# First stage of a decoder trunk reordered: modulation weights before the input rows, input rows in groups of two tiles, projections begun on half the tokens

## What is computed

```python
def rmsnorm(x, g):
    xf = x.astype(jnp.float32)
    y = xf * lax.rsqrt(jnp.mean(xf * xf, axis=-1, keepdims=True) + EPS)
    return (y * g.astype(jnp.float32)).astype(x.dtype)

c_act = jax.nn.silu(c)
for l in range(DEPTH):                                   # DEPTH = 2
    mod = c_act @ w_ada[l] + b_ada[l]                    # 6 rows of 1024
    sh_m, sc_m, g_m, sh_f, sc_f, g_f = [m[:, None, :] for m in jnp.split(mod, 6, axis=-1)]
    h = rmsnorm(x, norm_mix_g[l]) * (1 + sc_m) + sh_m
    if l % 2 == 0:
        z = h @ w_in_even[i]                             # 1024 x 2560
        u, v, b_gate, c_gate, x_in = jnp.split(z, split_pts, axis=-1)
        y_a = chunk_sgu(u, v, sgu_norm_g[i], w_spatial[i], b_spatial[i])
        y_b = short_gated_conv(b_gate, c_gate, x_in, conv_w[i])
        y = jnp.concatenate([y_a, y_b], axis=-1) @ w_out_even[i]
    else:
        y = pool_mixer(h, w_pool[i], pool_scale[i])
    x = x + g_m * y
    h = rmsnorm(x, norm_ffn_g[l]) * (1 + sc_f) + sh_f
    x = x + g_f * hier_moe(h, ...)                       # 32 experts, top 2
return rmsnorm(x, final_norm_g)
```

## Time and profile before

| | us |
|---|---|
| median of three runs | 1866.48 (1862.36 to 1868.59) |
| the profiled execution | 1867.46 |
| its span, first to last instruction | 1865.7 |
| PE busy | 1648.7 (88%) |
| DVE busy | 1567.1 (84%) |
| ACT busy | 1030.0 (55%) |

### The profile page before, as it was taken

How to read it: one execution, slowest core, us unless ns; L and a number is a source line. 1 busy time by engine, 2 the same in 40 slices (tenths; PEclk the granted TensorE clock), 3 DMA queues, 4 the chain that set the end, 5 groups by cost and what they waited for, 6 DMA issues and landing times. The chain is left out here.

```text
span 1865.7 us, 20029 instructions
## 1 busy us (share of the span) xinstructions
PE 1648.7 (88%) x7821; PEld 1367.8 (73%) x7821; DVE 1567.1 (84%) x1153; ACT 1030.0 (55%) x838; POOL 424.7 (23%) x230
## 2 busy tenths in 40 slices
PE   3799998996599999999999858659999999999980
PEld 3577786785478888888888748648888888888870
...
GB/s 331 210 300 316 272 85 85 46 46 181 134 325 378 376 383 384 393 382 385 381 392 388 388 141 207 53 109 324 380 385 385 392 386 384 385 384 388 392 204 277
DMA packets 125269, 547.60 MB, mean 294 GB/s; under 512 B 24003, under 2 KB 42975, under 8 KB 76021
## 3 DMA queue, kind: packets, MB, share of 16 engines
...
...
## 5 line engine op out<-in xcount | busy, mean ns | idle before, releaser
L1276 DVE TENSOR_TENSOR unit_low<-unit,unit_high 128x2048 fp32r<-128x2048 f32 x384 | 856.0, 2283 | 27.3 <-ACT unit_high L907 26.7
L907 ACT ACTIVATE unit_high<-unit 128x2048 fp32r<-128x2048 f32 x384 | 735.3, 1915 | 36.7 <-DMA unit<-in_moe_w_up_dram 13.6
L1567 PE MATMUL ps<-unit_high,block_columns_high 128*128 128x512 f32 x1024 | 408.6, 399 | 9.5 <-DVE block_columns_low L1281 9.5
L1569 PE MATMUL ps<-unit_high,block_columns_low 128*128 128x512 f32 x1024 | 402.5, 393 | 0.0
L1568 PE MATMUL ps<-unit_low,block_columns_high 128*128 128x512 f32 x1024 | 402.4, 393 | 0.0
L704 POOL DMA_INDIRECT expert_rows<-y_out,assignment x64 | 179.7, 2808 | 833.2 <-DVE y_out L1308 820.3
L1567 PEld LDWEIGHTS ps<-unit_high,block_columns_high 128*128 128x128 f32 x1024 | 194.4, 190 | 49.6 <-DVE block_columns_low L1281 10.8
L1569 PEld LDWEIGHTS ps<-unit_high,block_columns_low 128*128 128x128 f32 x1024 | 194.4, 190 | 41.8
L1568 PEld LDWEIGHTS ps<-unit_low,block_columns_high 128*128 128x128 f32 x1024 | 194.7, 190 | 39.0
L1579 PE MATMUL ps<-unit_high,act_columns_high 128*128 128x512 f32 x512 | 206.7, 404 | 9.8 <-DVE unit_low L1276 9.8
L1581 PE MATMUL ps<-unit_high,act_columns_low 128*128 128x512 f32 x512 | 201.6, 394 | 0.0
...
## 6 DMA issues: line engine op xcount, KB each, us to landing
unit<-in_moe_w_gate_dram SPq DMA_DIRECT2D x128, 1024.0 KB, 7.5
unit<-in_moe_w_up_dram SPq DMA_DIRECT2D x128, 1024.0 KB, 7.2
unit<-in_moe_w_down_dram SPq DMA_DIRECT2D x128, 1024.0 KB, 8.4
...
```

What stands on the lines that cost most here:

```text
L907: a.activation(high[k][:, :], raw[i % SLOTS][:, :], ACT.Copy).then_inc(unit_high, 1)
L1276: v.tensor_tensor(low[i % SLOTS][:, :], raw[i % SLOTS][:, :], high[k][:, :].bitcast(F32), ALU.subtract)\
L1567: mm(dst, xT_hi[:, q, :], high[k][:, cols], start=q == 0, stop=False)
L1569: last = mm(dst, xT_lo[:, q, :], high[k][:, cols], start=False, stop=q == KD - 1)
```

## The change

- SP loads the eight channel blocks of the 2048 modulation columns first, each as one transfer with 8 KB for a partition, blocks 4 to 7 as DVE frees the four buffers, and only then x. The bias of these rows comes as columns, in one small transfer, so the accumulator needs no clearing by POOL.
- ACT squares and takes the root of two tiles at a time (`x_squares`); DVE, not ACT, scales the rows (`x_rows`). PE transposes a group of two tiles into banks 4 to 7 (`x_columns`), and ACT and DVE make `h_columns_high`, `h_columns` and `h_columns_low` of 256 tokens directly from these banks (`h_high`, `h_rest`). POOL has no share in it any more.
- The unit order is piece 0 and piece 1 on the first 512 tokens, then both on the last 512. PE transposes the fourth group between unit 0 and unit 1.
- The parts are loaded when the fourth group has been transposed.

```diff
-        cond0 = [at(f"cond0_w{q}", [P, 2, D], SD + q * 8 * KB) for q in range(4)]
+        cond0 = [at(f"cond0_w{q}", [P, 2 * D], SD + q * 8 * KB) for q in range(4)]
...
+        def x_cols(t, k):
+            return BANK[4 + k // 2][:, (k % 2) * 2 * P + (t % 2) * P:(k % 2) * 2 * P + (t % 2 + 1) * P]
+        def group_cols(k):
+            return BANK[4 + k // 2][:, (k % 2) * 2 * P:(k % 2 + 1) * 2 * P]
+        ORDER = [(0, 0), (1, 0), (0, 1), (1, 1)] + [(w, half) for w in range(2, PIECES) for half in range(2)]
...
+            sp.dma_start(vec_rows[2 * KD + 3 * KA:NVEC, :],
+                         b_ada[0, 0:2 * D].rearrange("(m p) -> m p", p=P)).then_inc(vec_loaded, 16)
+            ada0 = w_ada[0].rearrange("(k p) n -> k p n", p=P)
+            for k in range(KD):
+                if k >= 4:
+                    sp.wait_ge(acc0_ready, k - 3)
+                sp.dma_start(cond0[k % 4][:, :], ada0[k, :, 0:2 * D]).then_inc(cond0_loaded[k % 4], 16)
             for i in range(4):
                 sp.dma_start(xr[:, 2 * i:2 * i + 2, :], xv[:, 2 * i:2 * i + 2, :]).then_inc(x_loaded[i], 16)
-            sp.wait_ge(acc_init, 1)
-            sp.dma_start(acc0[0:1, :], b_ada[0:1, 0:2 * D]).then_inc(cond0_loaded[0], 16)
-            ada0 = w_ada[0].rearrange("(k p) n -> p k n", p=P)
-            for q in range(4):
-                sp.dma_start(cond0[q][:, :, :], ada0[:, 2 * q:2 * q + 2, 0:D]).then_inc(cond0_loaded[q], 16)
-            for q in range(4):
-                sp.wait_ge(cond0_used, q + 1)
-                sp.dma_start(cond0[q][:, :, :], ada0[:, 2 * q:2 * q + 2, D:2 * D]).then_inc(cond0_loaded[q], 16)
             for w in range(RING):
                 load_piece(sp, w)
...
-            sp.wait_ge(acc_init, 2)
+            sp.wait_ge(acc_init, 1)
+            sp.wait_ge(x_T, GROUPS)
             for n in range(len(PARTS)):
                 part_loads(n)
...
-            piece_low(0)
-            for k in range(1, KD, 2):
-                pool.wait_ge(h_dve, h_made(k))
-                g.tensor_tensor(h_lo[:, k, :], hT[:, k, :], h_hi[:, k, :].bitcast(F32), ALU.subtract).then_inc(h_pool, 1)
-            for w in range(1, PIECES):
+            for w in range(PIECES):
                 piece_low(w)
...
+            def x_squares(i):
+                act.wait_ge(x_loaded[i], 16)
+                for t in (2 * i, 2 * i + 1):
+                    ch.link(a.activation(x_sq[:, :], xr[:, t, :], ACT.Square, accum_out=ss[:, X_IN, t:t + 1]))
+                root(X_IN, 2 * i, 2 * i + 2).then_inc(x_ss, 1)
+            def h_high(g):
+                cols = slice(2 * g * P, 2 * (g + 1) * P)
+                act.wait_ge(x_T, g + 1)
+                if g == 0:
+                    act.wait_ge(mod_ready0, 1)
+                for b in range(KD // 2):
+                    for k in (2 * b, 2 * b + 1):
+                        last = a.activation(h_hi[:, k, cols], group_cols(k), ACT.Identity, scale=a_m[:, k:k + 1],
+                                            bias=mod_c[:, SH_M, k:k + 1])
+                    if b % 2:
+                        for k in (2 * b, 2 * b + 1):
+                            last = a.activation(hT[:, k, cols], group_cols(k), ACT.Identity, scale=a_m[:, k:k + 1],
+                                                bias=mod_c[:, SH_M, k:k + 1])
+                    last.then_inc(h_act, 1)
             def piece_high(w):
                 act.wait_ge(piece_loaded[w % RING], 16 * (w // RING + 1))
                 a.activation(piece_hi[w % HRING][:, :, :], piece[w % RING][:, :, :], ACT.Copy).then_inc(w_high, 1)
...
+            x_squares(0)
+            x_squares(1)
+            h_high(0)
+            x_squares(2)
+            h_high(1)
+            x_squares(3)
             piece_high(0)
...
             piece_high(1)
+            h_high(2)
+            h_high(3)
...
+            def x_rows(i):
+                dve.wait_ge(x_ss, i + 1)
+                ch.link(v.reciprocal(rstd[:, X_IN, 2 * i:2 * i + 2], sd[:, X_IN, 2 * i:2 * i + 2]))
+                for t in (2 * i, 2 * i + 1):
+                    v.tensor_scalar(xr[:, t, :], xr[:, t, :], rstd[:, X_IN, t:t + 1], None, ALU.mult).then_inc(x_normed, 1)
+            def h_rest(g):
+                cols = slice(2 * g * P, 2 * (g + 1) * P)
+                for b in range(KD // 2):
+                    dve.wait_ge(h_act, 4 * g + b + 1)
+                    ks = (2 * b, 2 * b + 1)
+                    if b % 2 == 0:
+                        for k in ks:
+                            v.tensor_scalar(hT[:, k, cols], group_cols(k), a_m[:, k:k + 1], mod_c[:, SH_M, k:k + 1],
+                                            ALU.mult, ALU.add).then_inc(h_dve, 1)
+                    for k in ks:
+                        if b % 2 == 0:
+                            dve.wait_ge(h_dve, 4 * g + b + k % 2 + 1)
+                        v.tensor_tensor(h_lo[:, k, cols], hT[:, k, cols], h_hi[:, k, cols].bitcast(F32), ALU.subtract)\
+                         .then_inc(h_low, 1)
+            for k in range(KD):
+                dve.wait_ge(cond0_loaded[k % 4], 16 * (k // 4 + 1))
+                if k == 0:
+                    v.tensor_scalar(acc0[:, :], cond0[0][:, :], c_act[:, 0:1], None, ALU.mult).then_inc(acc0_ready, 1)
+                else:
+                    dve.wait_ge(acc0_ready, k)
+                    v.scalar_tensor_tensor(out=acc0[:, :], in0=cond0[k % 4][:, :], scalar=c_act[:, k:k + 1],
+                                           in1=acc0[:, :], op0=ALU.mult, op1=ALU.add).then_inc(acc0_ready, 1)
+            x_rows(0)
             dve.wait_ge(mod_cols0, 1)
...
+            ch.link(v.tensor_tensor(mod_c[:, :, :], PC[:, 0:2 * KD].rearrange("p (m k) -> p m k", k=KD), b_col, ALU.add))
             ch.link(v.scalar_tensor_tensor(out=a_m[:, :], in0=mod_c[:, SC_M, :], scalar=1.0, in1=vg_mix,
                                            op0=ALU.add, op1=ALU.mult))
             v.sem_inc(mod_ready0, 1)
...
+            x_rows(1)
+            h_rest(0)
+            x_rows(2)
+            h_rest(1)
+            x_rows(3)
+            h_rest(2)
+            h_rest(3)
...
+            def x_columns(g):
+                for t in (2 * g, 2 * g + 1):
+                    pe.wait_ge(x_normed, t + 1)
+                    for k in range(KD):
+                        if g and t % 2 == 0 and k % 2 == 0:
+                            b = k // 2
+                            pe.wait_ge(h_act, 4 * (g - 1) + b + 1)
+                            if b % 2 == 0:
+                                pe.wait_ge(h_dve, 4 * (g - 1) + b + 2)
+                        last = nc.tensor.transpose(x_cols(t, k), xr[:, t, k * P:(k + 1) * P], ident[:, :])
+                last.then_inc(x_T, 1)
+            x_columns(0)
             pe.wait_ge(vec_ready, 1)
...
+            pe.wait_ge(acc0_ready, KD)
+            for m in range(2 * KD):
+                last = mm(PC[:, m:m + 1], acc0[:, m * P:(m + 1) * P], ones[:, 0:1], start=True, stop=True)
             last.then_inc(mod_cols0, 1)
+            x_columns(1)
+            x_columns(2)
...
+            def project(u):
+                w, half = ORDER[u]
                 pe.wait_ge(w_low, w + 1)
...
+                if u >= 4:
+                    done = u - 3
+                    pe.wait_ge(*((proj_kept, done) if done <= 6 * KA else (z_kept, done - 6 * KA)))
+                tokens = slice(half * CH, (half + 1) * CH)
+                for k in range(KD):
+                    if u in (0, 2):
+                        pe.wait_ge(h_low, (2 * half + 1) * KD + k + 1)
+                    w_hi, w_lo = piece_hi[w % HRING][:, k, :], piece_lo[w % RING][:, k, :]
+                    mm(BANK[u % 4], w_hi, h_hi[:, k, tokens], start=k == 0, stop=False)
+                    mm(BANK[u % 4], w_hi, h_lo[:, k, tokens], start=False, stop=False)
+                    last = mm(BANK[u % 4], w_lo, h_hi[:, k, tokens], start=False, stop=k == KD - 1)
+                last.then_inc(proj_done, 1)
+                if u in PART_BEHIND:
+                    sum_part(PART_BEHIND[u])
             pe.wait_ge(mod_ready0, 1)
-            for w in range(PIECES):
...
+            for u in range(2 * PIECES):
+                if u == 1:
+                    x_columns(3)
+                project(u)
```

115 lines of the change are left out of this document (20 added, 95 removed).

## The result

| kernel | median, us | runs | lowest to highest | ratio to before, 95% interval |
|---|---|---|---|---|
| before | 1866.35 | 12 | 1862.36 to 1869.57 | |
| changed | 1875.91 | 12 | 1870.52 to 1878.19 | 1.0048 [1.0037, 1.0059] |

The changed kernel is slower by 0.48%, 6.9 to 11.0 us by the interval; the medians are 9.6 apart, the spans of the two profiled executions 10.1. The forecast was 12.0 us slower, 1878.5.

What follows compares the result with a forecast made beforehand. PE bounds the kernel behind the first stage, with DVE's chain of modulation parts close behind; its first part 14.2 us later, less 2.2 for its shorter length, makes 12.0 us slower: 1878.5 us, own range 1870 to 1885.

Steps and rivals of the forecast that it cites:

- First block of w_ada and first pair of x: Loads at the start: first block at 7.3 us, first x pair at 27.7, at 2.55 us per 1.05 MB transfer.
- Modulation columns: PE, after the second tile's transposes: 4.6 us as before, finished at 39.4 us.
- the 3 us that the reordering was to win: ACT's start on h: 40.0 us against 43.0 before, all that the new load order wins.
- ACT's 256-column operations: ACT's twelve operations per group of h: 0.50 us each, bounds 0.30 and 0.60, so 6.0 us a group.
- POOL and unit 0: POOL's low part takes 2.8 us; PE's first projection unit starts at 61.3 and takes 7.2, bounds 5.4 and 10.9.
- Part 0: First modulation part on DVE: starts at 77.4 us, 14.2 later than before, and takes 15.5 instead of 17.7.
- The later parts: Modulation parts behind the first on DVE: pace kept at 15.55 us each, sum of part 7 at 201.7, 12.0 later.
- The tail: Sums, units, gates and v behind the sum of part 7: move with it, 12.0 us later.
- one or two such falls more: Rival, PE's clock falling in new gaps before sums: one or two behind part 7 cost 1.7 us each, 1882; chance 0.12.
- the chain of parts catches up: Rival on DVE: parts at 14.0 us or less, PE's 4.0 us of waits go, 1864; chance 0.07.
- PE alone: Rival: the parts do not matter, PE enters the projections 1.4 us later, 1868; chance 0.06.
- PE's own side has room: PE between two sums: 12.8 or 18.2 us of own work, on average less than a part's 15.5.

Runs made afterwards that it cites:

- Experiment 1: Kernel before, with the loads of the later modulation parts held back until the second projection unit is done: 1877.1 us, ratio 1.0057.
- experiment 7: Changed kernel, each of the ten modulation parts loading and summing only four of its eight blocks: 1862.0 us, ratio 0.9986.
- experiment 8: Kernel before, each of the ten modulation parts loading and summing only four of its eight blocks: 1861.8 us, ratio 0.9976.
- experiment 12: Changed kernel with six instead of four buffers for the blocks of the modulation parts, nothing else: 1865.4 us, ratio 0.9988.
- experiment 3: Changed kernel with the modulation columns ahead of the first group's transposes on PE: 1872.6 us, ratio 1.0029.
- experiment 4: Changed kernel with x loaded ahead of w_ada again, and all squares and x_rows ahead of the modulation sums: 1877.3 us, ratio 1.0059.
- experiment 5: Changed kernel with modulation columns ahead of the first transposes, and all squares and x_rows ahead of the first operation on h: 1873.5 us, ratio 1.0037.
- experiment 2: Changed kernel with the transposes of the fourth group of x ahead of unit 0: 1874.4 us, ratio 1.0044.
- experiment 6: Experiment 5 plus the first modulation part's blocks loaded early into freed memory and summed between the groups of h: 1868.5 us, ratio 1.0019.
- experiment 9: Changed kernel with modulation columns ahead, the first modulation part loaded behind w_in with a semaphore per block, and six block buffers: 1857.0 us, ratio 0.9950.
- experiment 10: Kernel before with six instead of four buffers for the blocks of the modulation parts: 1860.5 us, ratio 0.9966.
- experiment 11: Changed kernel, its PE order kept, with the first modulation part loaded early and six block buffers: 1861.4 us, ratio 0.9982.

## Why the prediction was right, step by step

The mechanism held: part 0 must wait for x to be transposed whole, its late start goes through DVE to the sums on PE, and the reordering of the loads wins less than that costs. Experiment 1 shows that the late start suffices; 7, 8 and 12 show that most of the loss goes when the parts are shorter or faster. The sizes:

- *First block of w_ada and first pair of x.* 7.3 and 27.7 forecast; DVE starts at 7.36 and ACT at 27.32. The row of 411 GB/s carried this (426 in the changed kernel). By the 358 GB/s of the Trainium skill (DMA: Bandwidth & Descriptors, Specifications) ACT would have started 3.4 us later; neither row bears it out.
- *Modulation columns, mis-sized.* 4.6 us from the earlier trace rows; measured 6.83. There they followed 64 transposes, here 16 after 28 us of idle PE. The 16 transposes took 3.67 and not 2.06, so by the durations this stretch ran at the lower of the two clock levels, though the clock column reads 1.00 (see the last section). With the transposes, the way from the second scaled row (32.91) to the finished columns (42.59) took 9.7 us where 5.9 was forecast. This is the largest error at the start: h at 43.15 instead of 40.0. My own range had 2.0 us for it. So of the 3 us that the reordering was to win at ACT's wait for the modulation, none came (43.15 against 43.01).
- *ACT's 256-column operations.* 0.50 estimated, with bounds 0.30 and 0.60. Measured 0.45 from one to the next (four in 1.93, 0.58 each by themselves), so a group takes 5.4 to 5.6 and not 6.0; the two groups ahead of unit 0 gave about one microsecond back.
- *POOL and unit 0.* Unit 0 began at 63.3 (61.3 forecast) and took 8.1 us (7.2): its first twelve matmuls came 0.43 apart and the others 0.23. I had counted 8 of 24 as slow.
- *Part 0* at 79.63 instead of 77.4: the sum of the above. It took 95.11 - 79.63 = 15.5, as forecast.
- *The later parts* took (200.36 - 95.11) / 7 = 15.0 and not 15.55. That gave 3.6 us back by part 7: sum 7 is 10.65 later, where 12.0 was forecast. What decides between the two isn't shown: experiments 1, 3, 4 and 5 have 15.0 to 15.2, experiments 2 and 6, like the kernel before, 15.5.
- *The tail* moved by 9.0 and not with part 7. The sum of part 7 took 2.94 us before and 1.98 now. From its start to the last product of the convolution (4.75 us behind the last gates) 77.6 us pass in the kernel before, 77.5 to 77.7 in experiments 2 to 6 and 78.9 in experiment 1, but 75.9 to 76.0 in the changed one and in 7 to 12. The difference goes with a fall of PE's clock behind the wait for part 7: the granted clock of 190:225 is 0.95 before and in 2 to 6, 0.90 in 1, and 1.00 in the changed kernel. I had feared one or two such falls more; there was one less.

The errors, +2.2 at part 0, -3.6 in the parts and -1.7 in the tail, partly cancel: 12.0 - 3.1 = 8.9 us, and the last gates came 9.0 later (the medians are 9.6 apart). That the forecast came within 3 us is in part luck, for neither the faster parts nor the shorter tail was foreseen.

The rivals: "the chain of parts catches up" needed 14.0 us a part and did not come (15.0). With two buffers more it nearly does (13.9 in experiment 12, with 2.9 us of waits left), so its bound was real. I had set the floor of a part at 11.5; without any wait for DMA it is 13.55 at best and 14.1 in the mean (experiment 10), with products of up to 3 us beside POOL's low parts. "PE alone" priced the later entry at 1.4; it is 3.65, and by experiments 7 and 8 it puts the sum of part 7 3.55 later where the chain doesn't bind; in their times it shows as 0.3 us (medians) or 1.9 (ratios), uncertain by 3. That PE's own side has room held: its own pace is 93.96 / 7 = 13.4 us a part against 15.0 of the chain.

What stays open: behind that last product the profiled executions take 1594.8 to 1602.7 us to their end, in no order that goes with the kernels. So 8 us of scatter in the single profiled executions come from behind the change. The medians of single kernels carry some 2 us, and differences under 3 us are not argued from.
